# Raw x transposed at once, the first gather by token halves, and half of one expert unit loaded sooner: a block of mixer, cross-attention and 32 experts on one core

## The chip, the core and the metric

The kernel runs on one NeuronCore of a Trainium2 chip. The core has a matrix engine (PE, with its weight loads shown apart as PEld), a vector engine (DVE), an activation engine (ACT), a slower general engine (POOL), a sequencer for transfers (SP) and 16 DMA engines between HBM and the on-chip memory. Each engine runs its own instruction list in order; semaphores tie the lists together. The metric is device microseconds of one execution. Three runs of the kernel before took 664.26, 664.78 and 666.75 us, median 664.78.

## The reference

One block of a transformer-like model is computed for 256 tokens of width 1024, all in float32:

```python
h = h + hybrid_mixer(rms_norm(h, norm_mix), ...)            # RG-LRU (512) beside attention (8 heads of 64)
h = h + memory_cross_attention(rms_norm(h, norm_cross), mem, ...)   # 4 heads of 256, 256 memory rows
h = h + hier_moe(rms_norm(h, norm_ffn), ...)                # 4 groups of 8 experts, top 2
return rms_norm(h, norm_final)

def rms_norm(x, g):
    return x * rsqrt(mean(x * x, axis=-1) + EPS) * g
# mixer: proj = xn @ w_in ; x_lru, g_lru, q, k, v = split(proj)
```

1/rms is one number per token. A projection is linear, so it may be applied to the tokens before `x @ w_in`, or to the rows of the product. All 32 experts' weights (6 MB each, 201 MB together) are read, whichever experts the tokens choose.

## The kernel before

**Two phases.** The dense phase runs the mixer, the cross-attention and the routing. Its weights arrive as 30 halves of 1 MB, in the order of the list `STREAM` (two halves for each name: 0 and 1 are x_lru, 2 and 3 are q, 4 and 5 k, 6 and 7 v, 8 and 9 g_lru, and so on). ACT rounds a half into a high part (`split_hi(m)`), DVE subtracts to get the low part (`split_lo(m)`), and PE multiplies high and low parts in three products. `channels` (line 586) makes channel-major results such as xl0, xl1 (x_lru), gl0, gl1 (g_lru); `tokens` (line 601) makes token-major ones such as q0, q1. Activations are split in the same way when they have been transposed on PE: `turned_hi` on ACT and `turned_lo` on DVE.

**Expert phase.** 32 experts in 8 groups of 4. A group's tokens are gathered by matmuls with a selection matrix `ntake` (line 857: 24 instructions, then 8 more after the first half of the first expert), copied by DVE into `xg`, and taken through gate-up (line 885) and down (line 916). The weights lie in a ring of 12 units of 2 MB, three for each expert of a group: `EXPERT_UNITS = [(9, 10, 11), (6, 7, 8), (0, 1, 2), (3, 4, 5)]`. SP fills the ring the first time as memory of the dense phase comes free, and from then on refills each part as soon as PE has used it. `refill(1, False)` begins with a wait for the first half of group 0's first gate-up:

```python
sp.wait_ge(gu_used, 4 * BATCH * g + (4 * (j - BATCH) + 2 * part + 2))
```

**Memory shared by the phases.** The ring lies over the dense phase's buffers: units 0 and 1 over the landing place of raw weights, 2 to 4 over their split parts, 5 and 6 over the split activations, 7 to 10 over work space. So unit 5 is loaded when the last matmuls of the cross-attention's output projection (xo2, xo3) have read their activations.

**The start.** SP loads x in two halves of 128 tokens, the constants and parameters `ctab`, weight halves 0 and 1, mem, half 2, and so on. ACT sums the squares of x, POOL raises the mean to the power -0.5 (1/rms), ACT and DVE scale one token half each into `xtok`, PE transposes that into the four banks Tx0 to Tx3, ACT and DVE split it with the gain `norm_mix`, and PE multiplies by x_lru. POOL makes the low part of one half of weight half 0.

**Around the mixer.** DVE computes 26 small steps on `lambda` (lines 1403 to 1418), the convolution (lines 1432 and 1434) and `split_lo(5)`, in that order in its list; later a scan (line 1474) and the two softmaxes of the attention. The y of the recurrent branch is split on DVE (line 1369) before PE multiplies it by `out_lru` (`tokens(14, ...)`).

**Routing.** For each half of the tokens DVE chooses experts (`choose`), PE counts ranks with a triangular matrix (rank0, rank1), DVE writes the ranks (`place`, lines 1694 and 1697) and the selection matrix (lines 1704 and 1709). PE opens the four output sums with `open_sum` (line 774) between them. A count over all tokens ("over") guards a rare path that is not taken here.

**Banks.** `JOBS` lists the results in order; each takes the next of 8 PSUM banks in turn, or the one that `LATE` names, and waits until that bank's earlier result has been read. `LAST_JOB` names, for each weight half, the result after which its split slot may be overwritten.

## Time and profile before

| | us |
|---|---|
| median of three runs | 664.78 |
| the profiled execution, whole | 664.22 |
| its span, first to last instruction | 662.4 |
| PE busy | 504.6 |
| DVE busy | 234.2 |
| ACT busy | 181.6 |
| POOL busy | 20.7 |
| DMA share of 16 engines, queue of SP | 86.0% |

The page has one digit for each fortieth of the span (16.56 us). The last 25 digits, from 248 us on, show the DMA engines at nine tenths or more and 412 to 448 GB/s (but for the last digit). Before that the digits vary between 3 and 9. Busy shares over the whole span mix these two phases: PE is busy 45.00 of 45.00 us between 145 and 190 us, and 205.41 of 322 us between 340 and 662 us.

### The profile page before, as it was taken

To read this page: it belongs to the slowest core of one execution; us is meant where nothing else is said; L and a number is where in the kernel's file an instruction comes from. 1 tells how busy PE (TensorE), PEld (TensorE's weight loads), DVE (VectorE), ACT (ScalarE), POOL (GpSimd) and SP (SyncE) were. 2 spreads that over 40 slices of the span, in tenths; PEclk is the share of its full clock that TensorE was granted. 3 is DMA by queue.
4 is the path that set the end of the run, shared out by engine and by line. 5 is a ranking of instruction groups with operands and counts; after the bars stand their busy time and mean duration, and the time that the engine had idled before them with its cause. 6 is when DMAs were issued, how large, how long until landed. Compare 5 with 4: busy or idle time off the path is not lost.

```text
span 662.4 us, 13318 instructions
## 1 busy us (share of the span) xinstructions
PE 504.6 (76%) x5802; PEld 369.0 (56%) x5802; DVE 234.2 (35%) x518; ACT 181.6 (27%) x399; POOL 20.7 (3%) x21
## 2 busy tenths in 40 slices
PE   3999999999999887886656856666686666558654
PEld 3988998789888665654323523343353334335422
DVE  3796897664644632221111211121121112112203
ACT  6559567364442112120100011110001111000203
POOL 2000111200000000000000000000000000000000
PEclk9999999999999999999888977897897789889989
DMA  8655834396579799999999999999999999999993
GB/s 352 285 191 190 319 138 164 137 395 243 186 283 355 287 380 426 427 435 435 431 425 431 440 436 436 427 430 430 430 427 436 448 436 427 430 412 427 427 422 134
DMA packets 15716, 238.08 MB, mean 359 GB/s; under 512 B 1728, under 2 KB 1856, under 8 KB 3008
## 3 DMA queue, kind: packets, MB, share of 16 engines
q1 hardware_dynamic: 15536, 237.03, 86.0%
q8 instruction: 29, 0.48, 0.3%
q10 hardware_dynamic: 144, 0.52, 0.2%
q14 instruction: 7, 0.06, 0.0%
HBM read 236.49 MB, written 1.05 MB: 359 GB/s over the span
## 4 chain that ended last, share of the span: by engine, by line
PE 47%; DMA 45%; DVE 3%; ACT 2%; issue 1%; another core or an unknown queue 1%; POOL 1%; SPq 0%; ACTq 0%; DVEq 0%
DMA ring<-in_w_expert 44%; PE psum L610 15%; PE psum L596 11%; PE psum L885 9%; PE psum L916 4%; PE psum L857 1%; DMA landing<-in_dense 1%; PE psum L767 1%; PE psum L744 1%; PE psum L579 1%; PE psum L844 1%; PE psum L909 1%; DVE small L1769 1%; DVE small L1771 1%
## 5 line engine op out<-in xcount | busy, mean ns | idle before, releaser
L885 PE MATMUL psum<-ring,xg 128*32 128x256 f32 x2048 | 152.4, 459 | 90.9 <-DMA ring<-in_w_expert 84.6
L885 PEld LDWEIGHTS psum<-ring,xg 128*32 128x32 f32 x2048 | 73.6, 130 | 158.0 <-DMA ring<-in_w_expert 90.6
L610 PE MATMUL psum<-split_w,split_act 128*128 128x512 f32 x432 | 101.9, 393 | 1.2 <-DVE res L1544 1.2
L610 PEld LDWEIGHTS psum<-split_w,split_act 128*128 128x128 f32 x432 | 80.3, 188 | 18.4 <-DVE res L1544 1.6
L1230 ACT ACTIVATE small<-psum 128x128 f32<-128x128 f32 x32 | 8.9, 278 | 284.1 <-PE psum L885 284.1
L1769 DVE SCALAR_TENSOR_TENSOR small<-small,psum 128x128 f32<-128x128 f32 x32 | 9.2, 288 | 203.8 <-ACT small L1230 203.8
L1356 DVE TENSOR_TENSOR split_w<-landing,split_w 128x2048 fp32r<-128x2048 f32 x29 | 66.2, 2289 | 30.9 <-ACT split_w L1031 30.9
L596 PE MATMUL psum<-split_act,split_w 128*128 128x256 f32 x576 | 70.1, 284 | 1.1 <-DVE split_act L1369 1.1
L1031 ACT ACTIVATE split_w<-landing 128x2048 fp32r<-128x2048 f32 x30 | 57.3, 1914 | 49.3 <-PE psum L610 26.0
L596 PEld LDWEIGHTS psum<-split_act,split_w 128*128 128x128 f32 x576 | 69.5, 192 | 1.8 <-DVE split_w L1390 1.3
L1780 DVE COPY ybuf<-psum 32x128 f32<-32x128 f32 x128 | 37.3, 291 | 74.5 <-PE psum L916 73.6
L1031 ACT ACTIVATE ybuf<-psum 32x128 f32<-32x128 f32 x128 | 34.2, 267 | 52.7 <-PE psum L916 51.9
L916 PE MATMUL psum<-ring,small 128*32 128x128 f32 x1024 | 31.3, 274 | 6.2 <-ACT small L1031 5.5
L857 PEld LDWEIGHTS psum<-ntake,res 128*128 128x128 f32 x256 | 32.0, 200 | 7.2 <-issue 7.0
L916 PE MATMUL psum<-ring,more_hidT 128*32 128x128 f32 x1024 | 31.5, 274 | 5.9 <-ACT more_hidT L1031 5.5
L909 PE MATMUL psum<-ctab,small 128*128 128x128 f32 x32 | 9.8, 305 | 33.0 <-DVE small L1771 33.0
L857 PE MATMUL psum<-ntake,res 128*128 128x128 f32 x256 | 33.7, 288 | 0.1
L1759 DVE TENSOR_TENSOR xg<-psum,ctab 128x512 f32<-128x512 f32 x16 | 11.1, 692 | 63.9 <-PE psum L857 63.9
L916 PEld LDWEIGHTS psum<-ring,more_hidT 128*32 128x32 f32 x1024 | 26.9, 110 | 9.8 <-ACT more_hidT L1031 8.4
L916 PEld LDWEIGHTS psum<-ring,small 128*32 128x32 f32 x1024 | 27.0, 110 | 9.2 <-ACT small L1031 8.4
L844 PE MATMUL psum<-ybuf,small 128*128 128x512 f32 x64 | 29.8, 605 | 0.8 <-DVE ybuf L1780 0.8
L909 PEld LDWEIGHTS psum<-ctab,small 128*128 128x128 f32 x32 | 4.4, 139 | 45.7 <-issue 38.1
(182 smaller groups left out, 342.8 us busy)
## 6 DMA issues: line engine op xcount, KB each, us to landing
ring<-in_w_expert SPq DMA_DIRECT2D x20, 6144.0 KB, 48.2
ring<-in_w_expert SPq DMA_DIRECT2D x23, 2048.0 KB, 34.3
landing<-in_dense SPq DMA_DIRECT2D x30, 1024.0 KB, 5.5
ring<-in_w_expert SPq DMA_DIRECT2D x26, 1024.0 KB, 8.2
res<-in_x SPq DMA_DIRECT2D x2, 512.0 KB, 3.6
work<-in_mem SPq DMA_DIRECT2D x1, 1024.0 KB, 11.7
ybuf<-in_late SPq DMA_DIRECT2D x1, 512.0 KB, 14.4
after_routing<-in_norm_final SPq DMA_DIRECT2D x1, 512.0 KB, 13.2
```

The lines of the kernel that those rows point to most:

```text
L596: i = mm(b[:, 256 * c:256 * c + 256], w[a][:, k, P * c:P * c + P], src[t][:, k, :], start=k == 0 and n == 0, stop=k == KC - 1 and n == 2)
L610: i = mm(b, src[t][:, k0 + k, P * h:P * h + P], w[a][:, k, :], start=first and k == 0 and n == 0, stop=last and k == CT - 1 and n == 2)
L844: mm(bank(ACC_BANKS[2 * h + cb]), give[:, P * h:P * h + P], ybuf[:, 512 * cb:512 * cb + 512], start=False, stop=True, skip_group_check=Tru ...
L857: i = mm(bank(GATHER + part)[:, P * k:P * k + P], res[:, h, P * c:P * c + P], ntake[:, h], start=h == 0, stop=h == NH - 1)
L885: i = mm(half[SLOTS * strip:SLOTS * strip + SLOTS], xg[:, CT * part + k, SLOTS * j:SLOTS * j + SLOTS], w[:, k, :, P * strip:P * strip + P] ...
L909: tr(bank(HY)[:, 256:256 + P], hid, ident).then_inc(hid_turned, 1)
L916: i = mm(bank((HY, GATHER)[side])[SLOTS * strip:SLOTS * strip + SLOTS, 0:P], hidTs[j % 2][:, SLOTS * k:SLOTS * k + SLOTS], w[:, side, k, P ...
L1031: return nc.scalar.activation(dst, src, ACT.Identity, scale=scale, bias=bias)
L1356: V.tensor_tensor(lo, raw(m, chunks_of(m)), hi.bitcast(F32), ALU.subtract).then_inc(w_lo, 1)
L1759: V.tensor_tensor(xg[:, CT * part:CT * part + CT], bank(4 + part).rearrange("p (c n) -> p c n", c=CT), param("norm_ffn")[:, CT * part:CT * ...
L1769: V.scalar_tensor_tensor(th, th, 1.0, half[:, 0:P], ALU.add, ALU.mult).then_inc(gu_half, 1)
L1780: i = V.tensor_copy(ybuf[SLOTS * j:SLOTS * j + SLOTS, at:at + P], bank((6, 4)[side])[r, 0:P])
```

## The change

- **x.** x is no longer scaled first. PE transposes raw x, each half of the tokens as it lands; both column tiles of x_lru are multiplied from the unscaled x. q, k and v are scaled when ACT copies them out of PSUM (a scale per partition). x_lru and g_lru are channel-major, so they need 1/rms along a row: DVE writes a diagonal matrix, PE multiplies it by ones (a new job "rows"), ACT copies the result to `rstd_rows`, and DVE multiplies xl0, xl1, gl0 and gl1 by it (`times_rstd`). Before, ACT copied xl0, gl0, gl1 and DVE xl1.
- **First loads.** `ctab` is loaded in two parts: the identity and the parameters (200 columns) from ACT's queue, the other 581 columns from SP's, behind weight half 1. Weight half 0 lands in two pieces with a semaphore each. mem is transposed behind q.
- **First group.** The tokens are gathered by halves: 16 of the 32 matmul instructions (8 blocks, two instructions each) when the first half's selection is known, the rest after. Rank numbers are kept one higher, so that one DVE step falls away. Two `open_sum` and the count "over" move behind parts of the first expert.
- **Unit 5.** The activations of xo0 to xo3 are laid out by token half, so the first half of unit 5 is loaded when xo2 is complete; before, both halves waited for the last matmul of xo3.

```diff
...
-for _name, _cols in (("ident", P), ("before", P), ("causal", S), ("ones", P), ("iota", EXPERTS),
-                     ("cos", NH * HALF_ROT), ("sin", NH * HALF_ROT), ("power", 4)):
+for _name, _cols in (("before", P), ("causal", S), ("ones", P), ("iota", EXPERTS + 1),
+                     ("cos", NH * HALF_ROT), ("sin", NH * HALF_ROT), ("power", 4), ("ident", P)):
     CONSTS[_name] = (sum(n for _, n in CONSTS.values()), _cols)
 N_CONSTS = sum(n for _, n in CONSTS.values())
+FIRST = CONSTS["ident"][0]
...
+JOBS += [("rows", 1)]
+JOBS += [(f"q{h}", 1) for h in range(2)]
 JOBS += [(f"Tm{c}", 2) for c in range(4)]
-JOBS += [(f"q{h}", 1) for h in range(2)] + [(f"k{h}", 1) for h in range(2)]
+JOBS += [(f"k{h}", 1) for h in range(2)]
...
+        rstd_rows = scratch(8, 3088, S)
+        rstd_diag = scratch(8, 3344, S)
...
+        by_half = split_act[:, 0:UNIT].rearrange("p (h s c t) -> p s c h t", h=NH, s=2, c=KC)
+        os_ = tuple(by_half[:, part] for part in range(2))
...
                 sp.dma_start(res[:, h], x_in[:, h]).then_inc(x_loaded[h], 16)
-            sp.dma_start(ctab, early).then_inc(early_loaded, 16)
-            load_half(0)
+            sp.dma_start(landing[:, 0:HALF // 2], dense[0][:, 0:HALF // 2]).then_inc(raw_first, 16)
+            sp.dma_start(landing[:, HALF // 2:HALF], dense[0][:, HALF // 2:]).then_inc(raw_loaded[0], 16)
             load_half(1)
+            sp.dma_start(ctab[:, 0:FIRST], early[:, 0:FIRST]).then_inc(early_loaded, 16)
+            load_half(2)
             sp.dma_start(memraw, mem_in).then_inc(mem_loaded, 16)
-            load_half(2)
+            load_half(3)
             sp.dma_start(bd.rearrange("p c n -> p (c n)"), late[:, (KC + 1) * N_ROUTES:]).then_inc(bd_loaded, 16)
-            load_half(3)
             sp.dma_start(latetab, late[:, 0:(KC + 1) * N_ROUTES]).then_inc(router_loaded, 16)
-            sp.wait_ge(w_lo_first, 1)
...
             load_unit(2)
+            await_fill(sp, "xo2")
+            load_unit(5, (0,))
             await_half_used(sp, HALVES - 2)
             load_unit(3)
             await_half_used(sp, HALVES - 1)
             load_unit(4)
-            load_unit(5)
+            load_unit(5, (1,))
...
+            pe.wait_ge(first_loaded, 16)
+            for h in range(NH):
+                pe.wait_ge(x_loaded[h], 16)
+                for c in range(4):
+                    for k in range(2):
+                        i = tr(pb(f"Tx{c}")[:, 256 * k + P * h:256 * k + P * h + P],
+                               res[:, h, (2 * c + k) * P:(2 * c + k + 1) * P], ident)
+                    if h:
+                        end(i, f"Tx{c}")
+            for c in range(2):
+                begin(f"xl{c}")
+            pe.wait_ge(w_lo_first, 1)
+            for m, k0 in ((0, 0), (0, CT), (1, 0)):
+                w = slot(m, KC)
+                if m or k0:
+                    await_split(pe, m)
+                for c in range(2):
+                    for k in range(k0, KC if m else k0 + CT):
+                        if m == 0 and c == 0 and k % 2 == 0:
+                            await_read(pe, f"Tx{k // 2}")
+                        for n, (a, t) in enumerate(((1, 0), (0, 1), (0, 0))):
+                            i = mm(pb(f"xl{c}")[:, 256 * m:256 * m + 256], w[a][:, k, P * c:P * c + P], xs_[t][:, k, :],
+                                   start=k == 0 and n == 0, stop=k == KC - 1 and n == 2)
+                    if m:
+                        end(i, f"xl{c}")
+                if m == 0 and k0:
+                    i.then_inc(half_used, 1)
             pe.wait_ge(early_loaded, 16)
+            pe.wait_ge(diag_ready, 1)
+            end(mm(begin("rows")[:, 0:S], ones, rstd_diag, start=True, stop=True), "rows")
+            tokens_whole(2, ["q0", "q1"], xs_)
             pe.wait_ge(normed_act, 1)
             pe.wait_ge(normed_dve, 1)
-            turn("Tx", xtok)
-            channels(0, "xl0", xs_, "Tx")
-            channels(1, "xl1", xs_)
-            pe.wait_ge(normed_act, 2)
-            pe.wait_ge(normed_dve, 2)
             turn("Tm", memraw)
...
+            GATHER, HY, GU = 4, 6, 7
+            def gather_first(h, part, ks):
+                for k in ks:
+                    c = CT * part + k
+                    i = mm(bank(GATHER + part)[:, P * k:P * k + P], res[:, h, P * c:P * c + P], ntake[:, h],
+                           start=h == 0 and k == 0, stop=h == NH - 1, skip_group_check=True)
+                if h and ks[-1] == CT - 1:
+                    i.then_inc(gathered, 1)
+            pe.wait_ge(first_taken, 1)
+            for part in range(2):
+                gather_first(0, part, range(CT))
             pe.wait_ge(chosen, 2)
             end(mm(pb("rank1")[:, 0:EXPERTS], const("before"), picked[:, 1], start=False, stop=True), "rank1")
-            GATHER, HY, GU = 4, 6, 7
-            for h in range(NH):
-                await_read(pe, f"route{h}")
-                await_read(pe, f"rank{h}")
-            picked_all = rt(4)
-            begin("over")
-            for h in range(NH):
-                i = mm(pb("over")[:, OVER:OVER + EXPERTS], ones, picked_all[:, h], start=h == 0, stop=h == NH - 1)
-            end(i, "over")
+            def count_all():
...
+            def rest_and_count():
+                gather_first(1, 1, range(2, CT))
+                count_all()
+            def first_group():
+                pe.wait_ge(taken, 1)
+                gather_first(1, 0, range(CT))
+                gather_first(1, 1, range(2))
+                for h in range(NH):
+                    await_read(pe, f"route{h}")
+                gate_up(0, 0, 0, rest_and_count)
+                pe.wait_ge(late_sumsq, 2 * NH)
+                open_sum(0, 1)
+                await_read(pe, "over")
+                finish_expert(0, 0, 0)
+                gate_up(0, 1, 0)
+                open_sum(1, 1)
+                finish_expert(0, 1, 0)
+                for j in range(2, BATCH):
+                    expert(0, j, 0)
+                for cb in range(2):
+                    scatter(0, cb, range(NH))
...
-            group(0, 0)
+            first_group()
             group(1, 1)
...
+            nc.scalar.dma_start(ctab[:, FIRST:], early[:, FIRST:]).then_inc(first_loaded, 16)
+            act.wait_ge(x_loaded[0], 16)
+            sum_squares(res, 1, (0,))
+            act.wait_ge(first_loaded, 16)
+            turned_hi("Tx", xs_, "norm_mix", (0,))
+            hi = slot(0, KC)[0]
+            act.wait_ge(raw_first, 16)
+            copy(hi[:, 0:CT], raw(0, KC)[:, 0:CT]).then_inc(w_hi_first, 1)
+            turned_hi("Tx", xs_, "norm_mix", (1,))
+            act.wait_ge(raw_loaded[0], 16)
+            copy(hi[:, CT:], raw(0, KC)[:, CT:]).then_inc(w_hi, 1)
+            turned_hi("Tx", xs_, "norm_mix", (2, 3))
             split_hi(1)
+            act.wait_ge(x_loaded[1], 16)
+            sum_squares(res, 1, (1,))
+            split_hi(2)
             act.wait_ge(lambda_abs, 1)
             nc.scalar.activation(lru[:, 12:16], lru[:, 12:16], ACT.Exp, scale=-1.0).then_inc(lambda_exp, 1)
-            split_hi(2)
             act.wait_ge(mem_loaded, 16)
             sum_squares(memraw, 2)
+            split_hi(3)
...
+            await_fill(act, "rows")
+            release(copy(rstd_rows, pb("rows")[:, 0:S]), "rows")
...
+            dve.wait_ge(first_loaded, 16)
+            turned_lo("Tx", xs_, "norm_mix", (0, 1))
+            hi, lo = slot(0, KC)
+            dve.wait_ge(w_hi_first, 1)
+            V.tensor_tensor(lo[:, 0:CT], raw(0, KC)[:, 0:CT], hi[:, 0:CT].bitcast(F32), ALU.subtract).then_inc(w_lo_first, 1)
+            turned_lo("Tx", xs_, "norm_mix", (2,))
+            dve.wait_ge(w_hi, 1)
+            V.tensor_tensor(lo[:, CT:], raw(0, KC)[:, CT:], hi[:, CT:].bitcast(F32), ALU.subtract).then_inc(w_lo, 1)
+            turned_lo("Tx", xs_, "norm_mix", (3,))
+            split_lo(1)
             mean_squares(1)
-            scale_half(1, res, xtok)
-
-            dve.wait_ge(w_hi, 1)
-            hi, lo = slot(0, KC)
-            V.tensor_tensor(lo[:, 0:CT], raw(0, KC)[:, 0:CT], hi[:, 0:CT].bitcast(F32), ALU.subtract).then_inc(w_lo, 1)
-            dve.wait_ge(early_loaded, 16)
-            turned_lo("Tx", xs_, "norm_mix")
-            split_lo(1)
-
             V.scalar_tensor_tensor(lru[:, 12:16], param("lru_lambda"), -1.0, param("lru_lambda"), ALU.mult, ALU.max
                                    ).then_inc(lambda_abs, 1)
             split_lo(2)
+            dve.wait_ge(rstd, 1)
+            for h in range(NH):
+                i = V.tensor_scalar(rstd_diag[:, P * h:P * h + P], ident, stat[:, RS + h:RS + h + 1], None, ALU.mult)
+            i.then_inc(diag_ready, 1)
             mean_squares(2)
+            def times_rstd(job, dst):
+                await_fill(dve, job)
+                release(V.tensor_tensor(dst, pb(job).rearrange("p (c t) -> p c t", c=2),
+                                        rstd_rows.unsqueeze(1).to_broadcast([P, 2, S]), ALU.mult), job)
+            split_lo(3)
             scale_half(2, memraw, memraw)
+            await_read(dve, "rows")
+            times_rstd("xl0", xlp[:, 0::2, CONV - 1:])
+            times_rstd("xl1", xlp[:, 1::2, CONV - 1:])
...
+            times_rstd("gl0", gx[:, 0:2])
+            times_rstd("gl1", gx[:, 2:4])
             for t in range(CT):
...
-                V.tensor_scalar(rankm[:, h], rankm[:, h], -1.0, None, ALU.add).then_inc(rank_known, 1)
-                dve.wait_ge(rank_known, h + 1)
...
+            def first_slots(h):
+                for e in range(BATCH):
+                    i = V.tensor_scalar(ntake[:, h, SLOTS * e:SLOTS * e + SLOTS], iota[:, 1:SLOTS + 1],
+                                        rankm[:, h, e:e + 1], stat[:, RS + 6 + h:RS + 7 + h], ALU.is_equal, ALU.mult)
+                return i
             choose(0)
             add_xo("xo3", 1, 1)
             late_tokens("Tf4", 6, 2, 1)
             late_mean(1)
             place(0)
-            link(find_slots(0, 0))
-            slots_times_rstd(0)
+            first_slots(0).then_inc(first_taken, 1)
+            find_slots(0, 0)
             choose(1)
             place(1)
+            first_slots(1).then_inc(taken, 1)
             find_slots(1, 0).then_inc(slots_found, 1)
-            dve.wait_ge(slots_found, 1)
-            slots_times_rstd(1).then_inc(taken, 1)
...
+            take_gathered(0, 0)
             link(V.tensor_tensor(pick2, pick2, spread(e21, pick2), ALU.mult))
             link(V.tensor_tensor(by_group(gates), pick1, pick2, ALU.add))
+            dve.wait_ge(slots_found, 1)
+            give_gates(0)
+            take_gathered(0, 1)
+            dve.wait_ge(gtaken, 1)
```

Three places of the instruction lists. On DVE at the start of the program (Tx is split into `split_act`, the weights into `split_w`; `freed` counts a bank's readers), before:

```order
L1349 TENSOR_SCALAR stat<-stat 128x2 [waits sumsq]
L1365 TENSOR_SCALAR work<-res,stat 128x1024 [waits rstd]
L1390 TENSOR_TENSOR split_w<-landing,split_w 128x1024 [waits w_hi]
L1369 SCALAR_TENSOR_TENSOR split_act<-psum,ctab,split_act 128x256 [waits freed0,early_loaded]
L1369 SCALAR_TENSOR_TENSOR split_act<-psum,ctab,split_act 128x256
L1369 SCALAR_TENSOR_TENSOR split_act<-psum,ctab,split_act 128x256 [waits freed1]
```

and now:

```order
L1452 SCALAR_TENSOR_TENSOR split_act<-psum,ctab,split_act 128x256 [waits freed0,first_loaded]
L1452 SCALAR_TENSOR_TENSOR split_act<-psum,ctab,split_act 128x256
L1452 SCALAR_TENSOR_TENSOR split_act<-psum,ctab,split_act 128x256 [waits freed1]
L1452 SCALAR_TENSOR_TENSOR split_act<-psum,ctab,split_act 128x256
L1472 TENSOR_TENSOR split_w<-landing,split_w 128x1024 [waits w_hi_first]
L1452 SCALAR_TENSOR_TENSOR split_act<-psum,ctab,split_act 128x256 [waits freed2]
```

The wait for the sums of squares and for 1/rms is gone from the head of the list, and the first weight split now stands behind four operations on x. Later on DVE, where g_lru is complete (L1356/L1439 is `split_lo`, L1474/L1574 the scan, L1479/L1579 the first softmax), before:

```order
L1356 TENSOR_TENSOR split_w<-landing,split_w 128x2048 [waits w_hi] x2
L1474 SCALAR_TENSOR_TENSOR work<-work 128x256 x4
L1479 SCALAR_TENSOR_TENSOR work<-psum,ctab 128x4x128 [waits filled2]
L1479 SCALAR_TENSOR_TENSOR work<-psum,ctab 128x4x128 [waits filled3]
L1484 TENSOR_REDUCE soft<-work 128x8 [waits freed3,freed2]
```

and now:

```order
L1439 TENSOR_TENSOR split_w<-landing,split_w 128x2048 [waits w_hi] x2
L1491 TENSOR_TENSOR work<-psum,work 128x512 [waits filled0]
L1491 TENSOR_TENSOR work<-psum,work 128x512 [waits filled1]
L1574 SCALAR_TENSOR_TENSOR work<-work 128x256 x4
L1579 SCALAR_TENSOR_TENSOR work<-psum,ctab 128x4x128 [waits filled2]
L1579 SCALAR_TENSOR_TENSOR work<-psum,ctab 128x4x128 [waits filled3]
```

Two operations that wait for g_lru's two banks have come ahead of the scan. On PE at the first gather (L836/L884 is the count "over", L828/L876 the last rank, L885/L933 gate-up), before:

```order
L828 MATMUL psum<-small,ctab 128x32 [waits chosen]
L836 MATMUL psum<-small,ctab 128x32 [waits freed5,freed7,freed6]
L836 MATMUL psum<-small,ctab 128x32
L857 MATMUL psum<-ntake,res 128x128 [waits taken]
L857 MATMUL psum<-ntake,res 128x128 x11
L885 MATMUL psum<-ring,xg 32x256 [waits loaded9_1,loaded9_0,xg_ready]
```

and now:

```order
L867 MATMUL psum<-ntake,res 128x128 [waits first_taken]
L867 MATMUL psum<-ntake,res 128x128 x7
L876 MATMUL psum<-small,ctab 128x32 [waits chosen]
L867 MATMUL psum<-ntake,res 128x128 [waits taken]
L867 MATMUL psum<-ntake,res 128x128 x5
L933 MATMUL psum<-ring,xg 32x256 [waits loaded9_0,xg_ready,loaded9_1,freed7,freed6]
```

Between the wait for `taken` and the first gate-up there were 12 matmuls, and there are 6 (each is two instructions in the trace).

## Rows read from the trace of the kernel before

**Rows 1.** The page's second part: 40 slices of the span, GB/s moved.
```profile
GB/s 352 285 191 190 319 138 164 137 395 243 186 283 355 287 380 426 427 435 435 431 425 431 440 436 436 427 430 430 430 427 436 448 436 427 430 412 427 427 422 134
```

**Rows 2.** The chain that ended last: start us, us, what; its end.
```profile
601.86 47.18 DMA ring<-in_w_expert
```

**Rows 3.** Stretches of one us: length, PEclk, DMA share, GB/s.
```profile
219.00:220.00 1.00, 1.00 0.00 0
237.00:238.00 1.00, 1.00 0.17 66
```

**Rows 4.** SP's transfers in order of time: start us, us, engine, line, what, xcount.
```profile
222.08 1.84 SPq L444 DMA_DIRECT2D ring<-in_w_expert  x4
...
237.13 24.03 SPq L450 DMA_DIRECT2D ring<-in_w_expert  x10
```

**Rows 5.** The chain that ended last, at the dense phase's start.
```profile
13.92 11.87 PE psum L596 x96
25.79 1.75 PE psum L579 x16
27.54 21.88 PE psum L610 x96
```

**Rows 6.** Timeline from 5 to 17 us; in brackets idle before and its releaser.
```profile
5.31 1.06 ACT L1046 ACTIVATE small<-res 128x1024 f32<-128x1024 f32 x1 [0.16 <-DMA res<-in_x]
9.41 3.39 PE L579 MATMUL psum<-ctab,work 128*128 128x128 f32 x16 [9.41 <-ACT work L1031]
9.82 1.91 ACT L1031 ACTIVATE split_w<-landing 128x2048 fp32r<-128x2048 f32 x1 [0.51 <-DMA landing<-in_dense]
11.64 3.01 ACT L1031 ACTIVATE split_act<-psum,ctab 128x256 fp32r<-128x256 f32 x8
11.77 1.23 DVE L1390 TENSOR_TENSOR split_w<-landing,split_w 128x1024 fp32r<-128x1024 f32 x1 [2.91 <-ACT split_w L1031]
12.91 3.22 DVE L1369 SCALAR_TENSOR_TENSOR split_act<-psum,ctab,split_act 128x256 fp32r<-128x256 f32 x8
```

**Rows 7.** DVE's timeline, from the lambda steps to `split_lo(5)`.
```profile
24.81 0.17 DVE L1403 TENSOR_SCALAR lru<-lru 128x4 f32<-128x4 f32 x1
...
29.92 2.29 DVE L1356 TENSOR_TENSOR split_w<-landing,split_w 128x2048 fp32r<-128x2048 f32 x1
32.13 0.68 DVE L1383 COPY work<-psum 128x512 f32<-128x512 f32 x1
...
41.35 2.29 DVE L1356 TENSOR_TENSOR split_w<-landing,split_w 128x2048 fp32r<-128x2048 f32 x1
```

**Rows 8.** PE's and DVE's timelines between 75 and 106 us.
```profile
75.55 2.43 DVE L1474 TENSOR_TENSOR_SCAN work<-work 128x256 f32<-128x256 f32 x4
78.17 1.29 DVE L1479 SCALAR_TENSOR_TENSOR work<-psum,ctab 128x512 f32<-128x512 f32 x2 [0.19 <-PE psum L653]
...
95.03 2.29 DVE L1356 TENSOR_TENSOR split_w<-landing,split_w 128x2048 fp32r<-128x2048 f32 x1 [0.70 <-ACT split_w L1031]
...
102.18 2.70 DVE L1369 SCALAR_TENSOR_TENSOR split_act<-work,ctab,split_act 128x256 fp32r<-128x256 f32 x4 [1.86 <-ACT split_act L1031]
...
105.47 5.71 PE L610 MATMUL psum<-split_w,split_act 128*128 128x512 f32 x24
```

**Rows 9.** The chain that ended last, from the last rank to the first experts.
```profile
230.29 0.30 DVE ntake L1709
...
230.64 4.57 PE psum L857 x24
235.21 1.86 PE psum L885 x32
237.07 1.10 PE psum L857 x8
...
269.89 2.68 PE psum L857 x24
```

**Rows 10.** One us of PE: length, PE busy (instructions), PEclk, DMA share, GB/s.
```profile
231.00:232.00 1.00, 1.00 (x7) 0.50 1.03 434
```

131 lines of the change are left out of this document (67 added, 64 removed).

## The prediction

> **What bounds the kernel now.** I read the page's slices first, then the end of the chain of waits, then the transfers and the clock around 220 to 240 us, then the timelines of the start. The slices show 412 to 448 GB/s from 248 us to the last slice but one [rows 1], and the chain ends in waits for expert weights, the last one of 47 us [rows 2]. So the second phase is a stream of weights that runs at its rate whatever the engines do. Its end is the moment at which the first refill starts plus a constant. The first refill is issued at 237.13 us [rows 4], in the moment in which PE is through the first half of the first gate-up, 235.21 + 1.86 = 237.07 [rows 9]. Between 219 and 220 us nothing moves, and between 237 and 238 us only 66 GB/s [rows 3]: the DMA engines stand idle before the last units of the ring are asked for, and again for about one us when these have landed and the first refill is only being issued. Two things therefore count: how early PE reaches 237.07, and how many bytes of the first fill are still queued by then. Up to there PE is the chain, from its first real matmul at 13.92 on [rows 5], with little slack.
>
> **Start: what goes.** Before, x waited for its sums of squares and 1/rms, then PE transposed it, 9.41 to 12.80, then came the splits, and x_lru started at 13.92 [rows 5, 6]. Now the order is set by landings. The second half of x is there at 5.3 us. 1414 KB (ctab and weight half 0) landed behind it by 9.82, which is 314 KB/us [rows 6]; the steady stream does about 430 [rows 1]. The 102 KB on ACT's queue come ahead, 0.25 us, so the first 512 KB of the weight are there at 5.3 + 0.25 + 1.2 to 1.6 = 6.8 to 7.2. The transposes cost 3.39/16 = 0.21 us each; with the first eight done as the first tokens land, bank Tx0 is complete at about 6.3. ACT needs 3.01/8 = 0.38 for each piece of x: Tx0 until 7.15, half the weight (half of 1.91) until 8.2, Tx1 until 8.95. DVE needs 3.22/8 = 0.40 for each: Tx1 until 9.75, then 1.23 for the weight split that PE waits for, 11.0. PE starts at 11.1 in place of 13.92, a gain of 2.8 us. The POOL step that served weight half 0 is replaced by DVE and is ahead of PE's need, since 24 matmuls at 11.87/96 = 0.124 [rows 5] cover 3 us.
>
> **Start: what is added.** The "rows" matmul is two instructions; one of 512 columns costs 21.88/96 = 0.228 [rows 5], so at most 0.46. The diagonal needs both sums of squares and POOL; I place it at 19 us, 3 to 4 us before PE comes to it, and this slack hides it; beyond it each us would cost one. The transposes of mem only change places with q. That leaves 2.35 us.
>
> Next late is DVE. PE needs `split_lo(5)` behind q and half of k: 27.54 + 16.41 = 43.95; DVE has it at 41.35 + 2.29 = 43.64 [rows 5, 7], so DVE is only 0.3 us ahead. Now PE asks at 41.6. DVE starts the lambda steps, at 24.81 before, only after `times_rstd` on xl0 and xl1, which wait for "rows" (about 23.9) and for the scaling of mem: two operations like the copy of 0.68 [rows 7], until 25.9, thus 1.1 later. But `split_lo(3)` and the copy that stood from 29.92 to 32.81 [rows 7] are gone from the way: 2.9. DVE is done at 43.64 + 1.1 - 2.9 = 41.8 and PE, asking at 41.6, waits 0.2. About 2.1 us survive (bounds: 1.3 if mem or half 3 lands a us late; 2.35 if nothing waits).
>
> **The clock at the start.** Sixteen transposes of mem took 1.75 us, the sixteen of x at the very start 3.39 [rows 5, 6]: PE ran them at half speed, and x_lru after a gap of one us ran at full speed. Now the transposes end near 7.7, and PE idles for 3.4 us before 11.1. It may stand at half speed again and lose between nothing and 3.39 - 1.75 = 1.64. I take 0.5: the gap is longer than before, but the first 24 matmuls partly wait for splits anyway. The Trainium skill, page "TensorE: Matmul & The Clock Gate", section "What's actually happening", says that the slow state is the default and that activity releases it; this speaks against spreading PE's first work out, and the trace agrees as far as the slow transposes go. By that rule alone this term would be the whole upper bound.
>
> **g_lru.** ACT's copies become two DVE operations of about 0.68, and the second must wait until g_lru is complete, about 77.0. The scan started at 75.55 and the softmax at 78.17, waiting 0.19 for PE [rows 8]. Now the scan starts at 77.7 and the softmax at 80.1: DVE is 2.0 us later. Of that 0.7 disappears where DVE waited for ACT at 95.03, and about 0.3 in smaller waits. The low part of y was ready at 102.18 + 2.70 = 104.88, and PE took it at 105.47 [rows 8], so the slack is 0.6; 1.0 late makes a wait of 0.4 (bounds 0 and 1.4). Behind it PE and DVE are in step again. The dense phase therefore ends 2.1 - 0.5 - 0.4 = 1.2 us sooner.
>
> **First gather.** Before, DVE finished the selection at 230.59, PE gathered 24 instructions in 4.57 us and started gate-up at 235.21 [rows 9]. The same 24 cost 2.68 later [rows 9]; the granted clock was 0.50, which is 1.2 GHz, between 231 and 232 us [rows 10], after PE had mostly stood still while DVE chose. Now one rank step less and short selection steps (four of 32 columns for two of 128) put the start at 230.2 in before's times. 12 instructions remain ahead of gate-up, and DVE's copy to `xg`, about 0.7, lies beside the last four of them. The eight before it cost 0.9 at 2.68/24 = 0.112, or about 1.5 if the low clock sets in as before near 230.9. At full speed: 230.2 + 0.9 + 0.2 to drain + 0.8 = 232.1, end of the first gate-up half at 234.0. The 1.9 us lost before are nearly 4 us at half speed, from about 230.6 on; if they stand at the same time now, until 234.4, the first part of gate-up is slow too, 232.6 to 235.3. The gain is 3.1 or 1.8. I take 1.8, since PE's stand while DVE chooses is the same. The two `open_sum` and the count go behind gate-up, into the stretch in which PE waited for ACT and DVE, and behind the refill's trigger, so I cost them at nothing; were they exposed, they would delay the second refill, which has 4.9 us of the first 2 MB refill as cover.
>
> **Unit 5.** Its half now moves when xo2 is complete, into the idle time before 220. The first fill ends 1.05 MB/430 GB/s = 2.4 us sooner. By itself this gains nothing, for the refill waits for PE. But without it the stream would start again at 237.1 at the earliest, against 238.15 now, and would cap the gain of the gather at 1.0; with it the cap is 3.5.
>
> **Sum.** 1.2 + 1.8 = 3.0 us off the profiled execution's 664.22 (span 662.4 and 1.8 around it): 661.2. The median of the runs, 664.78, is 0.56 higher, so against it this is 0.54%. A measurement of this kernel tells about 0.5%, 3.3 us, from no change; my sum lies on that line. The copies by token half of xpv write the same number of elements: nothing, bounds 0 and 0.2.
>
> **Rivals.**
> - A, full clock in the first gather. PE's gather of the first tokens keeps it busy where `open_sum` did, and the list is shorter and shifted. For: the gap before `taken` shrinks by 0.4. Against: PE still stands over a us for `chosen`. Gain 1.2 + 3.1: 659.9.
> - B, the start is lost. The clock costs 1.64, and DVE's delay of 2.0 behind g_lru passes through but for the slack of 0.6. The dense phase gains 2.1 - 1.64 - 1.4, about nothing: 664.22 - 1.8 = 662.4. For: both slacks in rows 7 and 8 are under 0.7. Against: half of each must happen at its worst.
> - C, slower: PE runs all of x_lru at half speed, since short bursts of transposes and 24-matmul pieces behind splits do not bring the clock up. Price 11.87 us [rows 5] less the gains 2.1 - 0.4 + 1.8 = 3.5: 672.6. It decides from 3.5 us on, that is when 30% of the stage is slow. Against: x_lru ran at 0.124 each right after slow transposes.
> - D, the change does not do what it says for unit 5: its half queues behind the others and the stream is never shorter. Then the gather's gain is capped at 1.0: 662.0. Against: the idle us at 219 [rows 3].
>
> **Chances.** Forecast 0.45, A 0.20, B 0.22, C 0.07, D 0.06. Half of the forecast's spread, most of A and little of the rest lie beyond 0.5% faster: 0.47; within 0.5%: 0.45; slower by more: 0.08, which is C and an unforeseen wait. The range is 659.0 to 664.0; the forecast's own is 660.2 to 662.3.
>
> **What would show it.** The first x_lru matmul near 11.1 and its 96 in 11.9 to 13; q from 23.4 to 24; a short PE wait before k's second half and one near 104 for DVE's L1452; the first gate-up 3 us sooner than 235.21, with a granted clock of 0.50 beside it or not; no DMA gap at the first refill but the one us of issue; and the last 400 us alike. I am wrong if the first refill is issued later than 236 or earlier than 232, if the DMA engines show new gaps after it, or if PE stands at "rows".

## The result and the profile after

The changed kernel takes 671.63 us, the median of 4 runs (670.08 to 671.91). The kernel before took 665.46 in the same measurement (4 runs, 664.26 to 666.75), so the ratio is 1.0087, 95% interval 1.0068 to 1.0106. The change makes the kernel 0.9% slower. The prediction was 661.2 in a range of 659.0 to 664.0, and gave "slower" 0.08. It is wrong. Of all executions in this document one, of e4, ran in a slower state of the chip (853.96 us, mean granted clock 0.553), and the ratios leave it out.

The profiled execution took 670.08 us with a span of 668.3, which is 5.9 more than before. I followed one event after another through both traces. The table has the start in us of the same work.

| event | before | after | difference |
|---|---|---|---|
| first matmul of x_lru | 13.92 | 12.40 | -1.52 |
| matmuls of the lru's gates (L639, now L676) | 49.26 | 50.20 | +0.94 |
| first score matmul, behind g_lru (L653, now L690) | 76.98 | 77.92 | +0.94 |
| L682, now L719, behind g's last 96 matmuls | 102.93 | 108.36 | +5.43 |
| L813, now L850, behind xo3's matmuls | 221.89 | 229.04 | +7.15 |
| first refill issued | 237.13 | 243.34 | +6.21 |
| end of the span | 662.4 | 668.3 | +5.9 |

Three stages lose. From x_lru to the gates 2.5 us go, 2.1 of them in x_lru's 96 matmuls, which turns the lead of 1.5 into 0.9 late. From g_lru to L719 4.5 go, and ahead of L850 another 1.7. The first gather gives back 0.9. The last 400 us are as before: the GB/s slices of the changed kernel read like [rows 1].

```profile
GB/s 339 355 127 189 315 87 106 186 341 288 190 252 373 279 343 426 428 426 441 429 437 439 422 427 435 438 441 424 424 435 441 441 424 424 435 420 430 428 421 145
```

The chain that ended last of the changed kernel (start us, us, what), between 78 and 109 us:

```profile
78.03 0.69 DVE work L1491
78.72 6.97 DVE work L1574 x4
85.69 1.19 DVE work L1579 x2
...
93.01 2.21 DVE split_w L1439
...
95.26 13.26 PE psum L605 x96
```

L1574 is the scan, which took 2.43 us before [rows 8]. It takes 6.97 with the same four instructions and the same tiles. TensorE waits for VectorE's split, which comes behind the softmax, until 95.26. It then needs 13.26 for 96 matmuls, where the half of the same batch ahead of the stand took 11.77. What ran beside the scan shows in the timeline of POOL (GpSimd), and the spread of the scan's four in the view of that line (duration ns min/median/max):

```profile
78.89 2.12 POOL L1389 TENSOR_TENSOR work<-work 128x1024 f32<-128x1024 f32 x1 [57.53 <-DVE work L1491]
81.09 1.32 POOL L1391 TENSOR_SCALAR work<-work 128x1024 f32<-128x1024 f32 x1
82.50 2.65 POOL L1393 TENSOR_TENSOR work<-work 128x1024 f32<-128x1024 f32 x1
```

```profile
L1574 DVE TENSOR_TENSOR_SCAN work<-work x4: 681/1894/2818, 78.6 to 82.9; 128x256 f32<-128x256 f32 x4
```

The quickest instruction of the scan took 681 ns. The slowest took 2818, which is about 681 and one of GpSimd's operations (2.12 us). Before, the three operations of GpSimd started at 79.71, behind the scan. The change puts the two products with 1/rms, for which GpSimd waits, ahead of the scan, and so lets go GpSimd and the scan at the same moment.

One-us stretches of the changed kernel (length, PE, PEld, DVE, ACT, POOL busy, PEclk, DMA share, GB/s) show the two places where the granted clock is at its lower level of 1.2 GHz, and the stream ahead of the refill:

```profile
96.00:97.00 1.00, 1.00 (x7) 1.00 (x6) 1.00 (x1) 1.00 (x6) 0.00 (x0) 0.50 0.74 131
98.00:99.00 1.00, 1.00 (x7) 1.00 (x7) 0.97 (x3) 1.00 (x3) 0.00 (x0) 0.50 1.00 426
224.00:225.00 1.00, 1.00 (x4) 0.81 (x3) 0.86 (x5) 0.00 (x0) 0.00 (x0) 0.50 0.00 0
243.00:244.00 1.00, 1.00 (x15) 0.79 (x8) 0.04 (x1) 0.00 (x0) 0.00 (x0) 1.00 0.01 4
```

So the stage from g_lru to L719 loses 2.75 by the stand and 1.5 to 1.8 by the clock behind it, and xo3's 24 matmuls lose 1.6 (7.33 us in TensorE's timeline, where the same 24 took 5.73 before) by the clock alone.

The chain at the start of the changed kernel, beside [rows 5]:

```profile
1.64 6.85 DMA landing<-in_dense
...
8.52 1.06 ACT split_w L1109
9.57 0.74 ACT split_act L1109 x2
...
10.34 0.88 DVE split_act L1452 x2
11.21 1.14 DVE split_w L1472
...
12.40 13.96 PE psum L655 x96
26.36 0.44 PE psum L663 x2
```

TensorE starts at 12.40, and the 96 matmuls take 13.96 in place of 11.87. The granted clock reads 1.00 there, yet in the stretch from 16 to 17 us TensorE does 6 matmuls and from 18 to 19 it does 11 (the number in brackets behind PE's busy time):

```profile
16.00:17.00 1.00, 1.00 (x6) 1.00 (x6) 1.00 (x1) 1.00 (x1) 0.00 (x0) 1.00 1.12 451
18.00:19.00 1.00, 1.00 (x11) 1.00 (x10) 1.00 (x1) 0.96 (x1) 0.18 (x1) 1.00 0.99 410
```

The column is wrong there, and not the rate. In the trace of m2 (below), which runs the same start, the column does read 0.50 where TensorE does 6 to 7 matmuls a us:

```profile
15.00:16.00 1.00, 1.00 (x6) 1.00 (x6) 1.00 (x1) 0.97 (x3) 0.00 (x0) 0.50 1.03 422
```

The first gather, beside [rows 9], again from the chain:

```profile
237.12 0.72 DVE ntake L1823 x3
...
237.88 1.70 PE psum L867 x12
239.58 0.52 issue
240.10 3.18 PE psum L933 x32
```

From the gather's start to the refill's issue 5.46 us pass, where 6.49 did before.

### The profile page after: what moved, and what is told of

It reads as the page before. It is cut to its first block, busy times and chain, and to the rows that moved or that the text cites. A ratio compares the mean times of both kernels' runs of the same rounds, so it can differ in the third digit from the quotient of the medians.

```text
span 668.3 us, 13310 instructions
## 1 busy us (share of the span) xinstructions
PE 509.3 (76%) x5804; PEld 373.2 (56%) x5804; DVE 241.7 (36%) x527; ACT 179.9 (27%) x397; POOL 18.1 (3%) x20
## 4 chain that ended last, share of the span: by engine, by line
PE 45%; DMA 45%; DVE 6%; issue 2%; ACT 2%; POOL 1%; SPq 0%; POOLq 0%; ACTq 0%; DVEq 0%
DMA ring<-in_w_expert 44%; PE psum L622 15%; PE psum L933 9%; PE psum L605 7%; PE psum L964 4%; PE psum L655 2%; DVE work L1574 1%; PE psum L804 1%; PE psum L781 1%; DMA landing<-in_dense 1%; PE psum L590 1%; PE psum L892 1%; PE psum L957 1%; PE psum L905 1%; POOL stat L1380 1%
## 5 line engine op out<-in xcount | busy, mean ns | idle before, releaser
L933 PE MATMUL psum<-ring,xg 128*32 128x256 f32 x2048 | 150.2, 450 | 91.5 <-DMA ring<-in_w_expert 81.4
L933 PEld LDWEIGHTS psum<-ring,xg 128*32 128x32 f32 x2048 | 72.6, 128 | 157.3 <-DMA ring<-in_w_expert 87.0
L622 PE MATMUL psum<-split_w,split_act 128*128 128x512 f32 x432 | 103.8, 398 | 1.2 <-DVE res L1644 1.2
L1439 DVE TENSOR_TENSOR split_w<-landing,split_w 128x2048 fp32r<-128x2048 f32 x29 | 66.1, 2287 | 29.3 <-ACT split_w L1109 29.2
L1109 ACT ACTIVATE split_w<-landing 128x2048 fp32r<-128x2048 f32 (+1 forms) x31 | 57.6, 1861 | 44.1 <-PE psum L622 22.1
L605 PE MATMUL psum<-split_act,split_w 128*128 128x256 f32 x480 | 60.0, 288 | 2.7 <-DVE split_w L1439 2.7
L605 PEld LDWEIGHTS psum<-split_act,split_w 128*128 128x128 f32 x480 | 59.4, 196 | 3.4 <-DVE split_w L1439 3.0
L964 PE MATMUL psum<-ring,more_hidT 128*32 128x128 f32 x1024 | 33.2, 283 | 5.9 <-ACT more_hidT L1109 5.5
L1849 DVE TENSOR_TENSOR xg<-psum,ctab 128x512 f32<-128x512 f32 x16 | 11.1, 692 | 55.8 <-PE psum L905 52.6
L905 PEld LDWEIGHTS psum<-ntake,res 128*128 128x128 f32 x224 | 26.6, 192 | 6.2 <-issue 6.2
L905 PE MATMUL psum<-ntake,res 128*128 128x128 f32 x224 | 28.0, 278 | 0.0
```

What stands on the lines that cost most here:

```text
L605: i = mm(b[:, 256 * c:256 * c + 256], w[a][:, k, P * c:P * c + P], src[t][:, k, :], start=k == 0 and n == 0, stop=k == KC - 1 and n == 2)
L622: i = mm(b, tokens_of(src[t], k0 + k, h), w[a][:, k, :], start=first and k == 0 and n == 0, stop=last and k == CT - 1 and n == 2)
L905: i = mm(bank(GATHER + part)[:, P * k:P * k + P], res[:, h, P * c:P * c + P], ntake[:, h], start=h == 0, stop=h == NH - 1)
L933: i = mm(half[SLOTS * strip:SLOTS * strip + SLOTS], xg[:, CT * part + k, SLOTS * j:SLOTS * j + SLOTS], w[:, k, :, P * strip:P * strip + P] ...
L964: i = mm(bank((HY, GATHER)[side])[SLOTS * strip:SLOTS * strip + SLOTS, 0:P], hidTs[j % 2][:, SLOTS * k:SLOTS * k + SLOTS], w[:, side, k, P ...
L1109: return nc.scalar.activation(dst, src, ACT.Identity, scale=scale, bias=bias)
```

## The experiments

My theory after the two traces was: the scan and GpSimd's products take turns, instruction by instruction; this costs 4.6 us on VectorE, of which 2.75 reach TensorE, and the stand brings the half clock. The rivals were VectorE's lateness by the two added products alone, some other cause for the slow scan, and the clock's phases. All ratios are to the kernel before; medians of before were 665.5 to 665.9 in these measurements.

**e1: GpSimd behind the scan.** One line is added to the changed kernel.

```
+            pool.wait_ge(scanned, 1)
             nc.gpsimd.tensor_tensor(gate_r, gx, gx, ALU.mult).then_inc(pool_step, 1)
```

> The changed kernel, with GpSimd's gate work of the lru (three products behind g_lru) held back until VectorE's scan is done. Theory (the scan and GpSimd's products stand in each other's way, since the change puts g_lru's products with 1/rms ahead of the scan and so the scan beside GpSimd): the scan takes 2.4 us again instead of 7.0, softmax starts about 4.5 us sooner, TensorE's stand of 2.75 us before L605's 96 matmuls at 95 us goes and with it the half clock that cost 1.75 us: 671.6 - 4.5 = 667.1 us. Rival 1 (VectorE is only late because of the two added products, 1.4 us, and the scan is slow for another reason, its inputs or place): scan stays near 7 us, time 671 to 672. Rival 2 (the whole loss is the clock at the start and luck of its phases): no change either, 671 to 672.

Measured: 664.24 us, ratio 0.9987 (0.9973 to 1.0). The timelines of VectorE and of GpSimd have

```profile
78.08 2.43 DVE L1575 TENSOR_TENSOR_SCAN work<-work 128x256 f32<-128x256 f32 x4
```

```profile
80.68 1.90 POOL L1390 TENSOR_TENSOR work<-work 128x1024 f32<-128x1024 f32 x1 [59.38 <-DVE work L1575]
```

and TensorE runs 192 matmuls from 80.19 in one piece of 23.30 us. A single wait takes 7.4 us off in the medians and 6.6 between the two spans. This is more than the 4.5 expected; the trace of e1 has no half clock at xo3 either (L850 is at 222.26), and this gives the next 1.6, but m1 and e10 below have that half clock without the slow scan, so that it hangs on the scan is not shown. With the scan alone again, the change costs nothing against the kernel before.

**e2: the scan first.** The changed kernel with `times_rstd("gl0", ...)` and `times_rstd("gl1", ...)` moved from ahead of the four `tensor_tensor_scan` to behind them.

> The changed kernel, with VectorE's scan put ahead of the two products with 1/rms of g_lru. Theory: GpSimd can't begin before those products, so the scan runs alone at 2.4 us, the stand at 95 us goes: about 667.0 us, and since VectorE would be waiting for g_lru's second sum anyway while it scans, softmax starts even some tenths sooner than with GpSimd held back. Rival 1: the scan is slow by itself in the changed kernel (7 us): 671 to 672. Rival 2: the loss was the clock's phases: 671 to 672.

Measured: 664.52 us, 0.9983 (0.9971 to 0.9996); scan 2.43 from 75.96. This too is less than the 667.0 expected. It is the better repair, since VectorE scans while it would wait for g_lru, but in time the two can't be told apart.

**b1 and b2: the loss put into the kernel before.** b1 makes the scan wait until ScalarE has read both sums of g_lru. b2 does the same and holds GpSimd back behind the scan.

```
+            await_read(dve, "gl0")
+            await_read(dve, "gl1")
             for t in range(CT):
                 i = V.tensor_tensor_scan(xc[:, t], decay[:, t], root[:, t], 0.0, ALU.mult, ALU.add)
```

> The kernel before, with nothing of the change but this: the scan waits until ScalarE has read both of g_lru's sums, so that GpSimd's gate work runs beside it. Theory: the scan takes about 7 us instead of 2.43, VectorE comes to softmax about 6 us later (85 us instead of 78.2), TensorE stands for split_w before g's 96 matmuls and its clock falls: 665.0 + 4 to 5 = 669 to 670 us. Rival (slow scan comes from something else in the change): the scan keeps 2.43 us, VectorE only starts it 2 us later, TensorE does not stand: 665 to 665.5.

> The kernel before with the scan held back until ScalarE has read both of g_lru's sums (as in the earlier run that gave 672.3), and GpSimd's gate products held back behind the scan, so that the two do not overlap. Theory (the shared time of scan and GpSimd costs, 4.6 us, and TensorE stands only for what VectorE is late beyond some 4.8 us): the scan takes 2.43 us from 81.0, softmax starts near 83.6 instead of 88.1, TensorE stands at most 0.6 us before g: 666 to 667 us. Rival (the delay of the scan costs, whatever runs beside it): 671 to 672.

Measured: b1 672.28 us, 1.01 (1.0082 to 1.0117); b2 670.44, 1.0077 (1.0055 to 1.0098). VectorE's timelines and TensorE's, first b1's, then b2's:

```profile
81.04 7.06 DVE L1476 TENSOR_TENSOR_SCAN work<-work 128x256 f32<-128x256 f32 x4 [4.01 <-ACT work L1031]
97.67 14.28 PE L596 MATMUL psum<-split_act,split_w 128*128 128x256 f32 x96 [4.70 <-DVE split_w L1356]
```

```profile
79.59 2.44 DVE L1477 TENSOR_TENSOR_SCAN work<-work 128x256 f32<-128x256 f32 x4 [4.01 <-ACT work L1031]
79.75 23.63 PE L596 MATMUL psum<-split_act,split_w 128*128 128x256 f32 x192
107.35 5.74 PE L610 MATMUL psum<-split_w,split_act 128*128 128x512 f32 x24 [1.35 <-DVE split_act L1370]
```

b1 rebuilds the slow scan and the stand without any other part of the change: the scan takes 7 us again, TensorE stands at the same place, and the median rises by 6.7. But its scan also starts 5.5 us later than before, against 3.1 in the changed kernel, and so the stand is 4.70 and not 2.75. b2 parts lateness from taking turns. The scan is short again and the stand before g's second half is gone, as the theory had it, but a wait of 1.35 appears at the low part of y, and xo3 has the half clock (L813 at 225.38, 3.5 later than before). Its profiled execution took 667.65; four of its six runs took 670.2 to 671.3, and I can't say what these lose beyond it. So the theory's 666 to 667 was too low and the rival's 671 to 672 nearly right in the median. Lateness of 4 us on VectorE has a price of its own here, 4.6 us in the median, which my expectation left out, and only 1.8 us part the medians of b1 and b2, whose intervals overlap. So how much taking turns costs in the changed kernel rests on e1 and e2, and not on this pair.

**p1: taking turns by itself.** The kernel before, VectorE untouched, one more product on GpSimd beside the scan.

```
+            pool.wait_ge(w_lo, 12)
+            nc.gpsimd.tensor_tensor(gate_r, gate_r, gate_r, ALU.mult).then_inc(extra, 1)
```

> The kernel before with one more product on GpSimd (gate_r by gate_r, 128x1024, overwritten later) that is let go by split_lo(11), so that it runs beside the scan; the order and the start of everything on VectorE stay as they are. Theory (a GpSimd operation and a scan, both from and to SBUF, take turns whole instruction by whole instruction): one of the scan's four instructions takes 2 us longer, the scan 4.4 us in all instead of 2.43, or GpSimd's product takes longer by as much; softmax starts 2 us later, within VectorE's slack: 665.5 to 666.2. Rival (the long scans came from something else in g_lru's stage, such as ScalarE's or TensorE's reads at that place): scan 2.43 us, time 665.5.

Measured: 665.87 us, 1.0006 (0.9992 to 1.0021), VectorE's timeline and GpSimd's:

```profile
76.95 4.08 DVE L1478 TENSOR_TENSOR_SCAN work<-work 128x256 f32<-128x256 f32 x4
80.95 1.26 DVE L1483 SCALAR_TENSOR_TENSOR work<-psum,ctab 128x512 f32<-128x512 f32 x2
82.32 1.22 DVE L1488 TENSOR_REDUCE soft<-work 128x8 f32<-128x1024 f32 x1
83.45 2.48 DVE L1492 SCALAR_TENSOR_TENSOR work<-psum,ctab 128x512 f32<-128x512 f32 x4
```

```profile
77.17 2.14 POOL L1306 TENSOR_TENSOR work<-work 128x1024 f32<-128x1024 f32 x1 [53.20 <-DVE split_w L1360]
81.11 1.90 POOL L1310 TENSOR_TENSOR work<-work 128x1024 f32<-128x1024 f32 x1 [1.79 <-ACT work L1032]
83.09 1.05 POOL L1312 TENSOR_SCALAR work<-work 128x1024 f32<-128x1024 f32 x1
84.23 2.42 POOL L1314 TENSOR_TENSOR work<-work 128x1024 f32<-128x1024 f32 x1
```

The scan is 1.65 longer. The longest of its instructions took 2321 ns, where none took over 684 before. The next rows show the other half of the rule: VectorE's softmax steps, which read PSUM and one tile of SBUF, and its reduction run beside the very same GpSimd work at 2.48 and 1.22, as in the kernel before. The time doesn't move with the scan 1.65 us longer, so VectorE has that slack there. This settles why the scan is slow: GpSimd beside the scan lengthens it, whatever else stands in the kernel.

The Trainium skill has this rule. "SBUF — State Buffer", section "Who interferes with whom", says that a VectorE instruction with two SBUF inputs contends with a GpSimd instruction that reads SBUF, and that one with at most one SBUF input, outside the 2-port modes, does not. The same page, section "SBUF: two separate sides", says that whichever of the two starts first gets the shared ports for its whole instruction. The traces of the changed kernel (2818 ns) and of p1 (2321 ns) agree on the first half, and p1's 2.48 and 1.22 us on the second. "GPSIMD Engine Reference", section "1. Specifications", has the contention with two SBUF inputs in a row of its table.

**e3 and e4: extra matmuls at the start.** 20 matmuls into an unused bank, between x's transposes and x_lru, where TensorE stood 4.1 us; in the changed kernel (e3), and in e2 (e4).

```
+            for _ in range(20):
+                mm(bank(7)[:, 0:P], ident, ident, start=True, stop=True, skip_group_check=True)
             for c in range(2):
                 begin(f"xl{c}")
```

> The changed kernel with 20 extra matmuls (128x128, into a bank whose content is overwritten later) on TensorE between the transposes of x and the first of x_lru's matmuls, where it stands for 4.1 us. Theory of the start (x_lru's first 96 matmuls took 13.96 us instead of 11.87 because TensorE had stood before and came up at half speed): they take about 11.9 us again, all up to the scan comes 2.1 us sooner; the scan and its stand stay as they are: 671.6 - 2.1 = 669.5 us. Rival (x_lru is slow because its inputs, written in halves by two engines, arrive slowly): no change, or later by what the extra matmuls delay: 671.6 to 672.5.

> The changed kernel with the scan ahead of g_lru's two products with 1/rms, and with the 20 extra matmuls while TensorE waits for the first weights. Theory (the two losses, scan beside GpSimd and half clock at the start, are separate and add): scan alone gave 664.5, the start gives 1.5 (13.66 to 11.8 us for the first 96 matmuls, less what varies): 663.0 us, about 2.5 under before. Rival (what the start gains is lost again at the scan or in the next wait of VectorE, since VectorE and not TensorE then sets g_lru's stage): 664.5, as without the extra matmuls.

Measured: e3 670.28 us, 1.008 (1.0065 to 1.0095); e4 665.77, 1.0006 (0.9991 to 1.0021). TensorE's timeline of e3:

```profile
8.04 4.64 PE L644 MATMUL psum<-ctab 128*128 128x128 f32 x40
12.44 11.76 PE L657 MATMUL psum<-split_act,split_w 128*128 128x256 f32 x96
...
43.63 5.75 PE L622 MATMUL psum<-split_w,split_act 128*128 128x512 f32 x24 [0.88 <-DVE split_w L1441]
```

The matmuls of x_lru are back at 11.76, and so the 13.96 us come from TensorE's standing and not from late inputs. But of 2.2 us 0.88 are lost at once in a new wait for `split_lo(5)`, exactly where the prediction looked for 0.2. e3 took 1.35 less than the changed kernel, against 2.1 expected. Its first refill is issued at 239.37, 4.0 ahead of the changed kernel's, 1.6 of it at xo3 and 1.35 in the first gather, which both ran at the full clock in this execution, but its span is only 0.8 shorter. e4 (665.45 without the execution of 853.96, 663.0 expected) took no less than e2: the two gains don't add. The 20 matmuls hold x_lru's start back to 12.87, from 12.16 in e2, a wait of 0.28 comes at `split_lo(5)`, and the first refill is issued at 235.66, 0.65 ahead of e2's, but the span is 0.8 longer. Behind the refill e4 is 1.4 us longer than e2, and this lies at the very end: the last part of the result lands 5.0 us after its issue in e4 and 5.3 in e3, where it takes 3.5 or 3.6 in e2, the changed kernel and the kernel before. No run shows why.

**u1, u2, u3: the later parts alone.** The kernel before with its old start, and: gather by token halves and half of unit 5 sooner (u1); the gather alone (u2, which keeps the layout of xo's activations by token halves); unit 5 alone (u3). u1 and u3 load unit 5 in two halves:

```
+            await_fill(sp, "xo2")
+            load_unit(5, (0,))
...
-            load_unit(5)
+            load_unit(5, (1,))
```

> The kernel before with the two later parts of the change (first group's gather by token halves, half of unit 5 sooner), x scaled and transposed at the start as before. Theory (the later parts give what the traces of the changed kernel and of the run with GpSimd held back show from the first gather's start to the refill, 1.0 to 1.3 us, and nothing else changes): 665.6 - 1.2 = 664.4 us. Rival (VectorE's changed order of the selection costs as much as the gather gains): 665.6.

> The kernel before with the gather by token halves alone, unit 5 loaded in one piece where it was. Theory of the prediction (the first fill of the ring, which ends about 1.0 us before the refill could start sooner, caps the gain): 665.6 - 1.0 = 664.6 us at most, and DMA engines with nothing idle ahead of the refill. Rival (the fill is no cap, as it ends with the same slack in all): as with unit 5, 664.4; the two can't be told by time, only by the DMA's idle stretch ahead of the refill.

> The kernel before with half of unit 5 loaded sooner, and the layout of the out-projection's input by token halves that goes with it. Theory of the prediction: the fill of the ring ends 2.5 us sooner and nobody uses that, 665.6 us (same). Rival (the earlier load takes bandwidth from another unit that TensorE waits for, or the layout's strides cost VectorE and ScalarE): 666.2 or more.

Measured: u1 664.54 us, 0.9981 (0.9966 to 0.9996); u2 664.66, 0.9988 (0.9975 to 1.0002); u3 665.54, 1.0006 (0.999 to 1.0021). The one-us stretches from 236 us, first u2's, then the changed kernel with the scan first:

```profile
236.00:237.00 1.00, 1.00 (x20) 0.63 (x24) 0.86 (x5) 0.00 (x0) 0.00 (x0) 1.00 1.28 512
237.00:238.00 1.00, 1.00 (x21) 0.44 (x10) 0.42 (x2) 0.04 (x1) 0.00 (x0) 1.00 0.92 324
```

```profile
236.00:237.00 1.00, 1.00 (x16) 0.81 (x8) 0.07 (x1) 0.00 (x0) 0.00 (x0) 1.00 0.04 16
```

u2 issues the refill at 234.58, 2.55 ahead of before, and ends its span at 662.5 against 662.4. The stream has no hole left. TensorE's views near the end show where the lead goes, first the kernel before's, then u2's (L885 and L902 are the last expert's gate-up, L850 and L867 eight filler matmuls behind it):

```profile
641.72 1.93 PE L885 MATMUL psum<-ring,xg 128*32 128x256 f32 x32 [1.41 <-DMA ring<-in_w_expert]
644.93 1.06 PE L850 MATMUL psum<-ctab 128*128 128x128 f32 x8
```

```profile
640.27 2.45 PE L902 MATMUL psum<-ring,xg 128*32 128x256 f32 x32 [1.96 <-DMA ring<-in_w_expert]
644.08 1.92 PE L867 MATMUL psum<-ctab 128*128 128x128 f32 x8
```

The last gate-up starts 1.45 sooner, so 1.1 of the 2.55 are lost in the stream: that is the cap, which the prediction put at 1.0 of gain. The other 1.5 go behind it, at a granted clock of 0.50 that the kernel before doesn't have there. With unit 5 split the hole is there again. u3 changes nothing, as said. u1 and u2 can't be told apart by time; their medians are 0.9 and 0.8 under the kernel before's, and u2's interval reaches 1.

**e9, e8, e10: VectorE's order mended.** Two more moves on VectorE beside e2's. The first weight split goes ahead of the low part of x's second piece, and the lambda steps go ahead of `split_lo(3)`, where VectorE stood 3.0 us. e9 is that, e8 adds 10 extra matmuls at the start, and e10 six more ahead of the wait for `chosen`.

```
-            turned_lo("Tx", xs_, "norm_mix", (0, 1))
+            turned_lo("Tx", xs_, "norm_mix", (0,))
             ...
             V.tensor_tensor(lo[:, 0:CT], ...).then_inc(w_lo_first, 1)
-            turned_lo("Tx", xs_, "norm_mix", (2,))
+            turned_lo("Tx", xs_, "norm_mix", (1, 2))
```

> The changed kernel with three moves on VectorE and nothing else: the scan ahead of g_lru's products with 1/rms; the first weight split ahead of the low part of x's second piece; the lambda steps (23 short ones, 5 us) ahead of split_lo(3), where VectorE stood 3.0 us for ScalarE, instead of behind the products of x_lru. No extra matmuls. Theory (TensorE's first matmul waits for VectorE's order and not for a landing): x_lru starts at 10.9 instead of 12.4, its 96 take 13.5 to 14 us at the clock that it has, no wait at split_lo(5): 1.2 to 1.5 us less than with the scan alone moved (664.5), 663.2. Rival (the matmuls behind the first pieces wait for the next splits instead, and what starts earlier runs slower): 664.5.

> The same three moves, with 10 extra matmuls between x's transposes and x_lru, in TensorE's idle time. Theory (idle time ahead of x_lru brings the half clock, and VectorE no longer hides what that costs): x_lru from 10.9 in 11.8 us, another 1.8 us less than without the extra matmuls: 661.5 to 662. Rival (as in the earlier run with 20 extra matmuls, what the start gains ends in a wait for split_lo(5)): no less than without them, 663.2, with a TensorE wait of over 1 us near 41 us.

> The kernel of the previous run with 6 more extra matmuls where TensorE waits 1.3 us for VectorE's last choice before the first gather. Theory (the half clock in the first gather and gate-up, 12 and 32 instructions in 5.05 us where at full clock 3.53, comes from TensorE standing for VectorE just before): 3.5 to 4.0 us for the two, up to 1.5 us off the refill's time: 660.5. Rival (the half clock comes from the standing still earlier, or these matmuls only delay the rank step): no change against the previous run or 0.3 more.

Measured: e9 661.68 us, 0.9952 (0.9934 to 0.9971); e8 661.94, 0.9954 (0.9937 to 0.9972); e10 661.08, 0.9943 (0.9921 to 0.9965). All three beat both kernels. TensorE's timeline of e9:

```profile
10.39 13.33 PE L655 MATMUL psum<-split_act,split_w 128*128 128x256 f32 x96 [2.08 <-DVE split_w L1472]
...
229.04 1.97 PE L867 MATMUL psum<-ntake,res 128*128 128x128 f32 x12 [1.31 <-DVE ntake L1823]
231.25 3.03 PE L933 MATMUL psum<-ring,xg 128*32 128x256 f32 x32 [0.24 <-issue]
```

x_lru starts 2.0 us sooner than in the changed kernel, and the refill goes out at 234.34, 2.8 ahead of before; the span is 659.4, 3.0 shorter. The extra matmuls of e8 bring x_lru to 11.76 and the refill to 233.42, but the span behind it is 1.2 longer and the time stays. e10 has 1.60 and 1.93 for the first gather and gate-up, the full clock; m2, e3 and u2 had the same without extra matmuls there, so its matmuls aren't shown to be the cause, and its lead of 0.6 to 0.9 lies within the intervals. e9's theory asked for 663.2 and got 1.5 less. e8 lies in its expected 661.5 to 662 by luck, for its theory was 1.8 less than e9, and it is no less; here its rival is right on the time, though not on the wait. e10's 660.5 is missed by 0.6.

**m1 and m2: which of the moves.** m1 is e2 with the first weight split moved, m2 is e2 with the lambda steps moved.

> The changed kernel with the scan moved and the first weight split moved ahead of the low part of x's second piece; the lambda steps stay where the change has them. Theory (VectorE's lambda steps cap the start): x_lru starts at 10.9 us, TensorE then waits 0.5 to 1.0 us for split_lo(5) near 41 us: 0.6 to 0.9 less than with the scan alone, 663.7. Rival (the first split does all that the three moves did): 661.7 as in that run.

> The changed kernel with the scan moved and the lambda steps ahead of split_lo(3). Theory (TensorE, and not VectorE, is late at split_lo(5) as long as x_lru starts at 12.3 us and runs at the clock that it has): nothing, 664.5 as with the scan alone. Rival (the lambda steps did all that the three moves did): 661.7.

Measured: m1 661.76 us, 0.9953 (0.9934 to 0.9972); m2 664.6, 0.9987 (0.9972 to 1.0003). The first split's place does all of it; the lambda steps' place does nothing, and my cap of 663.7 for m1 was wrong by 1.9. m1's x_lru starts at 10.82, 1.3 ahead of e2's 12.16, and what makes the other 1.4 of the median isn't shown: the traced execution of m1 took 663.44, with the half clock at xo3. The wait for `split_lo(5)` is there in m1's trace, but it is 0.4 us (two batches of 48 in 11.60, where e9 has 11.16).

## Why the prediction was wrong, step by step

**The step that failed is g_lru.** It said "ACT's copies become two DVE operations of about 0.68", scan at 77.7, softmax at 80.1, "DVE is 2.0 us later", a wait of 0.4 with bounds 0 and 1.4. The scan started at 78.64, near enough. But the step took the scan's 2.43 from [rows 8] for its new place and did not ask what runs there. The two products also let GpSimd go, whose work stood behind the scan before. The scan took 6.97, the softmax started at 85.69, 7.5 late and not 2.0, and the stand came earlier than the place that I watched: at `split_w` before g's second half, 2.75 us, and 1.5 to 1.8 of half clock behind it. e1, e2, b1 and p1 show the mechanism from both sides. The rival B had the right stage with a price limited to 1.4, and C, the slower one, named the wrong place. No case held a slower VectorE instruction. C's 672.6 is near the measured 671.63 by luck: it wanted 11.87 us lost in x_lru, and 2.1 were. B's sum has a slip besides: 2.1 - 1.64 - 1.4 is 0.9 later and not "about nothing", so its time is 663.4. The sign "first refill later than 236" came true, at 243.34.

The trace of the kernel before already had a sign of the mechanism. The low part of y [rows 8] reads two tiles in SBUF, and one of GpSimd's operations runs beside it:

```profile
L1369 DVE SCALAR_TENSOR_TENSOR split_act<-work,ctab,split_act x4: 478/482/1504, 102.2 to 103.4; 128x256 fp32r<-128x256 f32 x4
```

```profile
103.09 1.51 POOL L1319 TENSOR_TENSOR work<-work 128x512 f32<-128x512 f32 x1 [17.84 <-ACT work L1144]
```

One of the four took 1504 ns where the least took 478, and its 2.70 us in [rows 8] hold this delay. It fits the same mechanism; no run takes GpSimd's operation away from there.

**The start.** Forecast: first matmul at 11.1, gain 2.8. Measured: 12.40, gain 1.52. The first 512 KB of the weight were to be there at 6.8 to 7.2 and landed at 8.5, 1.3 to 1.7 late, which is the whole difference of 1.3 at the first matmul. The rate is what was mis-sized: between 5.5 and 7 us the DMA engines moved 197 to 238 GB/s, where the step reckoned with 314 to 430 and the kernel before moved 333 to 402; why is not shown. What the step missed is that the late landing made VectorE's order wrong: the copy of the weight was ready at 9.57, and VectorE, then standing, took the low part of x's second piece first and waited for it until 10.34. Moving the split (m1 against e2) gives back 1.3 us at TensorE, and 2.8 in the median.

**The clock at the start.** Forecast 0.5, bounds 0 and 1.64. Measured 2.1 in the profiled execution, above the bound, since x_lru's matmuls paid for it and the bound was worked out from sixteen transposes. The rule of the Trainium skill's page "TensorE: Matmul & The Clock Gate" that was cited there ("What's actually happening": slow is the default, activity releases it) pointed the right way, and the trace agrees: 11.75 to 11.91 in all four runs with extra matmuls, 13.15 to 14.50 in the six with the new start and none. With the old start it is one or the other: 11.87 and twice 11.88, but 13.46 to 13.76 in b1, p1, u1 and u3. So 11.87 in [rows 5] was the luckier of two values, and with the new start only the other one was seen.

**Next late: `split_lo(5)`.** Forecast 0.2 of wait at a lead of 2.35. In the changed kernel TensorE was too late to wait. e3, with a start as fast as could be had, waited 0.88, and VectorE did the split at 41.29, no sooner than the 41.35 of [rows 7]. VectorE's chain was not 1.8 us sooner there, as computed. The 2.9 gone from its way were right: from the start of the lambda steps to the split 13.6 us pass, where 16.5 did. What was wrong is their start, forecast at 25.9 and measured at 27.7: VectorE stands 3.0 us for ScalarE's `split_hi(3)` ahead of them. m2, which puts the lambda steps into that stand, has the split at 39.11.

**First gather.** Forecast 1.8: start 0.44 sooner, the rest 1.36. Measured from the last rank step: the start is 0.1 later, since the four short steps of L1823 take 0.92, where three longer ones took 0.83 before; the rest gave 1.03. With e1's trace 1.3 and with m2's, at the full clock, 2.4. The size was somewhat off, the mechanism right, and rival A is one of its two values.

**Unit 5 and the cap.** Right. u2 ran into the cap by its trace, if not clear of noise by its time, and u3 gained nothing alone.

**The end as a constant behind the refill.** Right for this pair: 425.3 us before, 425.0 after, and 425.0 to 425.5 in e1, u1, u3, e9, e10, m1, b2 and p1. But it was 426.3 to 428.1 in e2, e3, e4, e8, m2, b1 and u2. The stream isn't at fault in most of them: from the first refill to the last expert's gate-up 404.1 to 404.6 us pass in all traces but u2's (405.7, the cap), e3's and b1's (405.0). The rest lies in the last expert, where e2, e4, e8, m2, u2 and b1 lose 1.0 to 2.5 us with TensorE at a granted clock of 0.50, and in the result's last transfer in e3 and e4. This is larger than several of the differences between these kernels. In number the forecast of 661.2 is near what the change gives with the scan and the first split in the right order (661.8, m1), but not term by term: the clock at the start took 1.3 there in place of 0.5, the gather gave 1.0 to 1.3 in place of 1.8 unless the clock was full, and m1's traced span is only 0.8 shorter than before.

## What to carry to other kernels

Where a step is moved on one engine, look also at what it releases on the others, and ask whether the released work reads SBUF beside a VectorE instruction with two SBUF inputs. A duration read from a trace holds only for the neighbours that it had there, and a maximum far above the minimum of like instructions (1504 against 478 ns) can be the sign of such a neighbour. In an engine's written order, put the operation that TensorE waits for ahead of those for later matmuls, and give each landing time a margin of over a us before relying on it. A stand of TensorE costs more than its length: here 2.75 us of wait drew another 1.5 to 1.8 of half clock, and the same happens at places that were not touched, so judge such changes by several runs.

## What the runs showed of the hardware that I had not expected

- A scan of 128x256 took 669 ns alone and up to 2818 ns beside GpSimd, and GpSimd's own operations grew only from 1.90, 1.06 and 2.41 to 2.12, 1.32 and 2.65. Here the loss fell on the engine with the short instructions: 4.6 us on VectorE against 0.7 on GpSimd.
- At the start TensorE ran at half speed (6 matmuls a us against 11) in stretches for which the profile's granted clock reads 1.00. Up to about 18 us that column can't be trusted in most of these traces; the rate of the instructions can. In the traces of m2 and e9 it reads 0.50 at the same rate.
- xo3's 24 matmuls took 7.2 to 7.3 us, with the clock at 0.50 for a part of them, in some executions (the changed kernel, b2, e10, m1) and about 5.7 in the others, with nothing near them changed.
